# Modulation products placed singly between the gate products of a convolution stage, with fewer row turns, the next weights split on GpSimd, and four stores

## The reference, cut to what matters

```
mods = silu(c) @ ada_w + ada_b                 # 9 vectors of 1024 a layer, for c and for c_ctx
u, g = split(h @ pw1_w + pw1_b)                # h: 512 tokens x 1024
u = u * sigmoid(g)
u = depthwise_conv(u, width 31) + dw_b         # per channel, 15 zeros at either side
u = layer_norm over channels;  y = silu(u) @ pw2_w + pw2_b
x = x + gate_vector * y
```

## Time and profile before

| | us |
|---|---|
| median of 3 runs | 3056.1 (3050.24 to 3059.17) |
| profiled execution | 3056.17, span 3054.4 |
| PE busy | 2897.7 (95% of the span) |
| DVE busy | 1628.0 (53%) |
| ACT busy | 1285.9 (42%) |
| POOL busy | 202.3 (7%) |
| granted PE clock, mean | 0.979 |
| loads | 1642 quarters of 256 KB, mean 145 GB/s |

### The profile page before, as it was taken

How to read it: one execution, slowest core, us unless ns; L and a number is a source line. 1 busy time by engine, 2 the same in 40 slices (tenths; PEclk the granted TensorE clock), 3 DMA queues, 4 the chain that set the end, 5 groups by cost and what they waited for, 6 DMA issues and landing times.

```text
span 3054.4 us, 51126 instructions
## 1 busy us (share of the span) xinstructions
PE 2897.7 (95%) x17674; PEld 2488.3 (81%) x17674; DVE 1628.0 (53%) x3043; ACT 1285.9 (42%) x2511; POOL 202.3 (7%) x150
## 2 busy tenths in 40 slices
PE   7999999999999999899998878999999999989998
PEld 7979789799788897788886545788877888768998
DVE  5566765655677656432335797423334333448655
ACT  4445444554554445432333444423334323335544
POOL 0001010000010100000001680000000000000000
PEclk9999999999999999999999998999999999989999
DMA  7556265555661655533333772333324233241553
GB/s 249 183 175 214 71 204 181 179 183 179 182 219 46 218 186 172 181 111 96 103 97 122 243 249 83 127 94 97 106 62 145 86 107 100 87 148 49 181 184 102
DMA packets 239198, 443.13 MB, mean 145 GB/s; under 512 B 26416, under 2 KB 27440, under 8 KB 238384
## 3 DMA queue, kind: packets, MB, share of 16 engines
q1 hardware_dynamic: 237632, 433.47, 44.7%
q0 software_dynamic: 1392, 7.34, 0.7%
HBM read 439.65 MB, written 1.05 MB: 144 GB/s over the span
## 4 chain that ended last, share of the span: by engine, by line
PE 82%; DVE 12%; POOL 2%; issue 2%; ACT 1%; DMA 1%; SPq 0%; DVEq 0%; ACTq 0%; POOLq 0%
PE ps L755 82%; DVE low L1820 2%; DVE ps L1823 2%; POOL hidden L2453 1%; DVE hidden L1823 1%; DVE zl L1823 1%; DVE hidden L1820 1%; DVE x L1826 1%; DVE coef L2367 1%; DMA raw<-weights 1%; POOL low L2414 1%; DVE hidden L2371 1%; DVE neg_max L2166 1%; DVE zl L1820 1%; DVE hidden L2193 0%
## 5 line engine op out<-in xcount | busy, mean ns | idle before, releaser
L755 PE MATMUL ps<-zh,low 128*128 128x256 f32 (+1 forms) x4192 | 1391.6, 332 | 78.3 <-DVE low L1820 40.9
L755 PE MATMUL ps<-zl,high 128*128 128x256 f32 (+1 forms) x4192 | 1380.5, 329 | 0.0
L755 PE MATMUL ps<-zh,high 128*128 128x256 f32 (+1 forms) x4192 | 1379.7, 329 | 0.0
L1820 DVE TENSOR_TENSOR low<-raw,high 128x512 fp32r<-128x512 f32 x1276 | 847.5, 701 | 429.9 <-ACT high L1355 427.4
L1355 ACT ACTIVATE high<-raw 128x512 fp32r<-128x512 f32 x1304 | 764.8, 625 | 593.8 <-PE ps L755 514.0
L755 PEld LDWEIGHTS ps<-zh,low 128*128 128x128 f32 x4192 | 805.5, 192 | 183.4 <-DVE low L1820 43.2
L755 PEld LDWEIGHTS ps<-zh,high 128*128 128x128 f32 x4192 | 805.7, 192 | 68.6
L755 PEld LDWEIGHTS ps<-zl,high 128*128 128x128 f32 x4192 | 806.3, 192 | 66.9
L1820 DVE TENSOR_TENSOR hidden<-gated,ps 128x256 f32 (+1 forms) x176 | 91.5, 520 | 602.7 <-ACT gated L1355 602.7
L1355 ACT ACTIVATE gated<-ps 128x256 f32<-128x256 f32 (+1 forms) x176 | 81.3, 462 | 493.7 <-PE ps L755 493.5
L755 PE MATMUL ps<-high,zl 128*128 128x512 f32 (+2 forms) x544 | 196.6, 361 | 3.8 <-DVE zl L1820 3.8
(11 more groups left out here) (202 smaller groups left out, 1938.5 us busy)
## 6 DMA issues: line engine op xcount, KB each, us to landing
raw<-weights SPq DMA_DIRECT2D x1642, 256.0 KB, 3.4
hidden<-norms POOLq DMA_DIRECT2D x4, 1024.0 KB, 6.3
cst<-consts SPq DMA_DIRECT2D x1, 1830.0 KB, 12.7
x<-x_in SPq DMA_DIRECT2D x1, 1024.0 KB, 5.9
x<-tokens_in POOLq DMA_DIRECT2D x1, 1024.0 KB, 12.4
x<-ctx_in POOLq DMA_DIRECT2D x1, 1024.0 KB, 6.4
out<-hidden POOLq DMA_DIRECT2D x1, 1024.0 KB, 5.1
```

The lines of the kernel that those rows point to most:

```text
L755: return nc.tensor.matmul(out, lhsT, rhs, start=first, stop=last, **kw)
L1820: return nc.vector.tensor_tensor(out, a, b, op)
```

## The change

In the convolution the fills of the first 13 fill places are no longer 8 products in a row: each single product stands between the triples of the gate and value products, one before each `mm3`. CONV_FILLS says which halves have one: none in group 0, the first half of group 1, both halves in groups 2 to 7. Five whole fills follow the last group. The stream is reordered to suit.

Fills are gathered in batches of 4, 4, 4 and 6. Those of one batch are accumulated in one bank, each in its own two of the 32 stationary columns (`cs` is 42 wide, and a window that moves by two selects them). The rows of a batch are turned once, with 2 times 4 or 6 columns of `row_sel`.

DVE splits the quarters of group 0 and of the first half of group 1 (now among the 8 quarters ahead), POOL all others of the convolution and the eight of `pw2`, which DVE split before. The gates of groups 1 to 3 are taken at other taps. The output is stored by SP in four DMAs of two tiles each.

```
+CONV_FILLS = ((0, 0), (1, 0), (1, 1), (1, 1), (1, 1), (1, 1), (1, 1), (1, 1))
+TAIL_FILLS = 5
+CONV_BATCHES = (4, 4, 4, 6)
 # stream()
-                    yield ("up_half", ("conv", 0), (t, a), 2, False)
-                    yield fills.pop()
-            yield fills.pop()
-            yield fills.pop()
+                    if CONV_FILLS[t][a]:
+                        _, m, g, _, _ = fills.pop()
+                        yield ("up_quarter", ("conv", 0), (t, a, 0), 1, False)
+                        yield ("ada_part", m, (g, 0, 1), 1, True)
+                        yield ("up_quarter", ("conv", 0), (t, a, 1), 1, False)
+                        yield ("ada_part", m, (g, 1, KT), KT - 1, True)
+                    else:
+                        yield ("up_half", ("conv", 0), (t, a), 2, False)
+            for _ in range(TAIL_FILLS):
+                yield fills.pop()
 # PE
+            def group_with_fill(self, n, a):
+                if self.in_batch == 0:
+                    self.turn_rows(7)
+                j, size = self.in_batch, BATCHES[self.fills]
+                first = self.q
+                parts = [first + 1] + list(range(first + 3, first + 2 + KT))
+                for g in range(2):
+                    at = first + 2 * g
+                    self.split += 1
+                    pe.wait_ge(low_ready, self.split)
+                    for i in range(4):
+                        k, f = 4 * a + i, 4 * g + i
+                        strip = slice(32 * i, 32 * i + 32)
+                        pe.wait_ge(landed[parts[f] % RING], 16 * (parts[f] // RING + 1))
+                        self.mm(ps[strip, 6, :], cs[:, f, 10 - 2 * j:42 - 2 * j], raw[:, parts[f] % RING, :], f < 4 and j == 0, f >= 4 and j == size - 1,
+                                skip_group_check=True).then_inc(amid_done, 1)
+                        w = (high[:, at % RING, i * P:i * P + P], low[:, at % RING, i * P:i * P + P])
+                        m = self.mm3(ps[:, 2 * (n % 2) + g, :], w, self.z(k, slice(0, 512)), k == 0, k == KT - 1, skip_group_check=True)
+                m.then_inc(quarter_done, 2 + KT)
...
                 for n in range(KT):
-                    if n >= 2:
-                        pe.wait_ge(conv_taken, seen.now(conv_taken) + n - 1)
                     for a in range(2):
-                        self.group([(ps[:, 2 * (n % 2) + g, :], True) for g in range(2)], 512, coming=coming if n == 0 else None, halves=(a,))
-                        self.fill(6, 7)
-                seen(conv_taken, KT)
-                self.fill(6, 7)
-                self.fill(6, 7)
+                        if n >= 2 and a == 0:
+                            pe.wait_ge(conv_taken, seen.now(conv_taken) + n - 1)
+                        if CONV_FILLS[n][a]:
+                            self.group_with_fill(n, a)
+                        else:
+                            self.group([(ps[:, 2 * (n % 2) + g, :], True) for g in range(2)], 512, coming=coming if n == 0 else None, halves=(a,))
+                for _ in range(TAIL_FILLS):
+                    self.fill(6, 7)
+                pe.wait_ge(conv_taken, seen(conv_taken, KT))
                 for k in range(KT):
+                    if k == 6:
+                        self.turn_rows(7)
                     self.stat(512, 0, z_ready, conv_out, k)
 # DVE, the taps
-                        if n == 0 and t == PAD - 1:
+                        if n == 0 and t == PAD:
                             next_gate(1)
-                        if n == 0 and t == TAPS - 2 or 0 < n < KT - 2 and t == TAPS - 6:
+                        if n == 1 and t in (first + 3, TAPS - 3):
+                            next_gate(2 if t == first + 3 else 3)
+                        if 1 < n < KT - 2 and t == TAPS - 6:
                             next_gate(n + 2)
-                        if n >= KT - 2 and t == TAPS - 4 or n == 0 and t in (3, PAD - 1, 17, 24, TAPS - 1) or 0 < n < KT - 2 and t in (first + 6, TAPS - 4):
+                        if (n, t) in ((0, 18), (1, TAPS - 6), (3, first + 8), (5, first + 8), (7, TAPS - 3)):
                             self.take_cols(7)
+                self.n += AHEAD
+                self.s = self.q + AHEAD
                 v.wait_ge(low_ready, self.n)
-                self.ahead(-6)
...
-                self.ahead()
                 v.wait_ge(dev_ready, seen(dev_ready, 4))
 # POOL
+            for i in range(AHEAD):
+                split(starts[4 * KT + i])
-            pool.wait_ge(result_ready, 1)
-            pool.dma_start(out, wide[:, :, 0:S]).then_inc(stored, 16)
-            pool.wait_ge(stored, 16)
 # SP
+            for i in range(4):
+                sp.wait_ge(result_ready, i + 1)
+                sp.dma_start(out[:, 2 * i:2 * i + 2, :], wide[:, 2 * i:2 * i + 2, 0:S]).then_inc(stored, 16)
+            sp.wait_ge(stored, 16 * 4)
```

More of the change, by code:

```diff
@@ L223, in stream, with fill_batches @@
     assert not fills
+def fill_batches():
+    kinds = ["conv" if kind == "up_half" else "ada" for kind, _, part, *_ in stream()
+             if kind in ("ada", "up_half") or kind == "ada_part" and part[1] == 0]
+    before = kinds.index("conv")
+    conv = sum(CONV_BATCHES)
+    return [1] * before + list(CONV_BATCHES) + [1] * (DEPTH * GROUPS - before - conv)
 def raw_quarters():
@@ L364, in build @@
     RAW = raw_quarters()
-    FILLS = DEPTH * GROUPS
+    BATCHES = fill_batches()
+    AMID = [at for at, kind in enumerate(kind for kind, _, _, n, _ in stream() for _ in range(n)) if kind == "ada_part"]
     with ExitStack() as stack:
@@ L1008, in pre_norm @@
                     self.fill_rows(6, range(begun, KT))
-                    if not early and (n, l) != (0, 0):
+                    if not early and self.turns < self.fills - 1:
                         self.turn_rows(7)
-                assert self.turns >= fills_before(l, n)
+                assert sum(BATCHES[:self.turns]) >= fills_before(l, n)
                 self.stream((4 if early else 1) if has_fill(n, l) else 12, 1)
@@ L1664, in conv, with half @@
                 w = c("conv_w").rearrange("p (k t) -> p k t", k=KT)
-                for n in range(2):
-                    while self.s < self.q + 2:
-                        self.next_high()
+                def half(n, a):
+                    for _ in range(CONV_FILLS[n][a]):
+                        self.fill(6, 7)
                     self.q += 2
[L1669 to L1674, removed]
+                half(0, 0)
+                half(0, 1)
+                self.next_high()
+                self.next_high()
+                self.gate_of(0)
+                half(1, 0)
+                half(1, 1)
+                self.gate_of(1)
                 self.next_high()
@@ L1704, in conv @@
                         self.next_high()
+                    if n < KT - 1:
+                        self.gate_of(n + 1)
+                for _ in range(TAIL_FILLS):
+                    self.fill(6, 7)
+                self.take_rows()
                 seen(conv_taken, KT)
@@ L2015, in pre_norm @@
                             self.ahead(k // 2 - 4)
-                if has_fill(n, l) and not early:
+                if has_fill(n, l) and not early and self.taken < self.fills - 1:
                     self.take_cols(7)
@@ L2335, in conv @@
                 self.by_tile = self.paired = True
-            def low_by_pool(self, n):
-                for q in range(self.q, self.q + n):
-                    assert not RAW[q] and q >= self.s - n
-                    if q >= self.s:
-                        self.n += 1
-                self.s = max(self.s, self.q + n)
             def attention(self):
@@ L2403, in _, with split @@
             pool.dma_start(x[:, :, S:512], tokens_in).then_inc(tokens_landed, 16)
-            first = 0
+            starts, at = [], 0
             for kind, key, _, n, _ in stream():
-                if key == ("conv", 0):
-                    break
-                first += n
-            starts = [first + (2 + KT) * h for h in range(2 * KT)]
+                if kind in ("up_half", "up_quarter") or key == ("pw2", 0):
+                    starts += range(at, at + n)
+                at += n
             def low_of(n, i):
-                q = starts[2 * n + i // 2] + i % 2
+                split(starts[4 * n + i])
+            def split(q):
                 pool.wait_ge(high_ready, sum(not a for a in RAW[:q + 1]))
```

142 lines of the change are left out of this document (89 added, 53 removed).

## The result

The changed kernel takes 3106.2 us (3105.5 to 3110.3, 4 runs), the kernel before 3054.4 beside it: ratio 1.0167, interval 1.0151 to 1.0184. It is slower by 51.9 us in the medians and by 49.3 in the spans (3054.4 to 3103.7); the forecast was +40.9. In a later session the same kernel took 3106.2 again (4 runs), against 3058.5, ratio 1.0157 (1.0138 to 1.0175), span 3103.5. One execution of an experiment's kernel (the pairs in two strips) took 7732 us at a mean granted clock of 0.55 and is left out of every figure.

What follows compares the result with a forecast made beforehand. DVE's taps bound the stage before; the change makes PE bound it. Last tap 44.2 us later, splits -1.3, stores -2.0: +40.9 on 3056.17, so 3097 us; own range 3083 to 3112, stated range 3066 to 3112.

Steps and rivals of the forecast that it cites:

- end of group 0 on PE: Entry of the convolution stage: PE finishes group 0's products at 1657.1 us, bounds 1655 to 1660.
- a single: One 32-column product between full ones on PE costs 1.17 us, streaming 0.88 plus switching; 104 cost 121.7.
- end of group 7 on PE: PE finishes the convolution's last group at 1861.8 us, against 1809.5 before the change.
- last gate to last tap: DVE's 45 taps after the last gate take 37.1 us, without the 6.0 wait for POOL, covering five whole fills.
- last tap to `pw2`: Between the last tap and `pw2`, moving six splits off DVE saves 1.3 us.
- stores: At the kernel's end, four 256 KB stores by SP instead of one of 1 MB save 2.0 us (1 to 3).
- everything behind, to the last scaling: From `pw2` to the last scaling: the prediction's sum had no term here, 0 us.
- the second rival: Convolution stage: switches are hidden, a single product costs only 0.88 us; 30 us less, 3067 us; chance 11%.
- the first: Convolution stage: single products run beside full ones or cost 0.23 us, DVE bounds; 3015 us, faster; chance 7%.
- the 18.9 us of waits for POOL are gone: Convolution stage: POOL's splits come before PE asks for them, so PE's 18.9 us of waits vanish.
- The third rival: Convolution stage: granted clock falls from 2.4 to 1.2 GHz; for half of 205 us, +100 us, 3197; chance 5%.

Runs made afterwards that it cites:

- the repeated execution: The changed kernel, unchanged, timed and profiled again in a later session: 3106.2 us, span 3103.5.
- experiment 1: The changed kernel with single products bunched: fours in four strips 3046.8 us, pairs in two strips 3053.1, pairs in one strip 3086.2.
- Experiment 2: The changed kernel with the counter that frees weight ring buffers raised in two steps: 3104.2 us, then 3103.4 beside 3106.2.
- experiment 4: The kernel before with only the four stores by SP, 3051.5 us (ratio 0.9989); with only POOL splitting `pw2`'s quarters, 3054.3 (0.9990).

## Why the prediction was right, and where it was off

The direction, the bound and the mechanism held; the size fell short by 49.3 - 40.9 = 8.4 us in the spans. The measured 3106.2 lies within the forecast's own range (3083 to 3112), but for neither of the reasons that its upper end stood on: a single did not cost 1.25 us, and the loads were not late.

| step | predicted | measured |
|---|---|---|
| end of group 0 on PE | 1657.1 | 1657.1 |
| a single | 1.17 | 1.18 |
| end of group 7 on PE | 1861.8 | 1869.4 (gate 7's sigmoid 1869.46) |
| last gate to last tap | 37.1 | 38.3 (37.8 in the repeated execution) |
| last tap to `pw2` | -1.3 | -2.75 |
| stores | -2.0 | -3.6 |
| everything behind, to the last scaling | 0 | +2.8 |

- **The end of group 0** agrees to 0.1 us by luck: in eleven profiles it lies between 1654.0 and 1659.9, a scatter wider than the bounds that I gave (1655 to 1660).
- **The single's price** was right for the reason given. Three widths of bunch and one with no neighbour (experiment 1) show both of its terms, so the second rival (the switches hidden) is out, and the first (0.23 a product) comes near only where a visit fills four strips (1.18 / 4 = 0.30). The Trainium skill, page "TensorEngine Tiling (Array Packing)", Key Properties, says that changing the tiling mode drains the engine. The traces agree that each such visit costs extra, some 0.29 us; that it is a drain they can't show.
- **The step that failed** is the sentence "the 18.9 us of waits for POOL are gone". Of the 7.5 us by which group 7 ended late, 1.44 + 2.69 + 1.67 = 5.8 are such waits. I had reckoned POOL's place in its own queue and not what feeds it. Its `low` needs ACT's `high`; that needs a free ring buffer, which PE frees only at the end of a half; and one such `high` stands ahead of gate 0, another behind gate 1. Experiment 2 took two of the three away with one counter. Of the remaining 1.7 us, 1.0 is 104 x 0.01 and 0.2 the waits before three turns (0.78, not 0.7); the rest I can't divide.
- **Last gate to last tap**: DVE's taps had the durations given. The small operations of the modulation did not, as the timeline of DVE after shows, while POOL splits `pw2`'s quarters:

```profile
1905.09 1.21 DVE L1896 TENSOR_TENSOR mods<-mods_raw,cst 128x16 f32<-128x16 f32 x1
1906.33 1.19 DVE L1902 TENSOR_SCALAR mods<-mods 128x16 f32<-128x16 f32 x1
```

  The five whole fills behind the last gate were covered, at 385 GB/s in 1880 to 1900.
- **Splits**: 1.16 of the 1.3 were really there (experiment 4). The other 1.6 of the 2.75 was a fall of the clock in the profiled execution of before, which the prediction had not seen in its rows.
- **Stores** were mis-sized: I had taken a load's landing of 3.4 us for a store of 256 KB, and it is 2.4. The rest is the issuing instruction and what stands before it, 0.9 us, which I had left out (experiment 4). In the medians experiment 4 has 3.4, on the edge of no change.
- **Behind the stage** 2.8 us came on top. Some 1.6 of them are the clock at the next norm: the repeated execution, which didn't lose it, has 1178.2 us from the first `pw2` product to the end, and this one 1179.8. The rest wasn't traced. From the first `pw2` product to the end of the span the eleven profiles of experiments with four stores have 1175 to 1181 us, with no edit in that stretch but the dummies in three of them, so a term of 2 or 3 us here is not to be had from one profile.
- The third rival, the clock falling in the stage, did not come: 1.00 in every window of 20 us from 1640 to 1900. In the repeated execution it fell once in the stage, to 0.91 in 1680 to 1700, behind the wait of 2.69.

## What to carry to other kernels

A product that fills one strip of the array costs as much as four that fill them all, and each visit between full products pays its switch: fill the visit first, then place it (here 1.18 us each against 1.18 for four, 59 us in the time). After each such gain ask again who bounds: the stage went from DVE to PE to POOL and back to DVE, and the cheapest edit of all, two lines of order in POOL's queue, was worth 16 us once PE had room. A wait can cost PE twice, by itself and by the clock behind it, so read PE's busy time and clock as well as its idle time. Follow a wait back through every queue and every buffer's release before calling it gone.

## What the runs showed of the hardware

- The clock falls behind the same wait in some executions and not in others. Behind 2.69 us of idle PE it was 0.55 in one execution and 1.00 in the next of the same kernel, and it fell in six of the eleven profiles that have this wait; behind 1.27 us, 0.55 and 1.00 as well. Each fall, to the 1.2 GHz level for part of the stretch, cost about 1.6 us where nothing stood behind it, and nothing where PE had to wait next in any case.
- Two or four float32 products in strips of their own take no longer than one, both passes included: 0.99 against 0.97 us from the first start to the next full product.
- DVE operations of 16 columns took 1.1 to 1.3 us in place of 0.17 at several places where POOL was at work. Those read ended within 0.05 us of the end of the POOL operation beside them. After: at 1905.09 and 1906.33, ending at 1906.30 and 1907.52, where the last two of POOL's eight splits end at 1906.26 and 1907.49; 0.17 again at 1907.7. Before: at 1795.03, ending at 1796.24 (split 1796.21), and 0.17 at 1853.8, with POOL idle. It did not happen beside every POOL operation: before, at 1815.09, 0.17 beside a TENSOR_SCALAR on POOL.
- The taps of 512 columns, which read PSUM, kept their 0.75 to 0.76 beside POOL. The first tap of a group, which reads none, took 1.66 at 1817.4 with POOL adding and 0.76 at 1841.7 with POOL idle. Whether reading PSUM makes the difference was not tried.
